# Reordering the recurrent block's second half in a one-core, two-block transformer kernel

## The reference, cut to what matters

```
u = x @ w_in
gate, rec = u[..., :D_RNN], u[..., D_RNN:]
rec = causal_depthwise_conv(rec, conv_w, conv_b)        # 4 taps
g = einsum('bsnd,nde->bsne', rec by 8 blocks of 128, w_gate) + b_gate
r = sigmoid(g[..., :128]);  i = sigmoid(g[..., 128:])
log_a = -8 * r * softplus(-lam);  a = exp(log_a)
b = sqrt(-expm1(2 * log_a)) * (i * rec)
h_t = a_t * h_(t-1) + b_t                               # scan over tokens
out = (gelu(gate) * h) @ w_out                          # then added to the residual
```

## Time and profile before

| | us |
|---|---|
| Median of three runs | 1183.83 |
| Profiled execution, its own time | 1185.08 |
| Span in the profile | 1183.3 |
| TensorE (PE) busy | 1170.0 (99%) |
| VectorE (DVE) busy | 819.0 (69%) |
| ScalarE (ACT) busy | 691.8 (58%) |
| GpSimd (POOL) busy | 89.3 (8%) |
| Mean granted TensorE clock | 0.999 |

### The profile page before, as it was taken

How to read it: one execution, slowest core, us unless ns; L and a number is a source line. 1 busy time by engine, 2 the same in 40 slices (tenths; PEclk the granted TensorE clock), 3 DMA queues, 4 the chain that set the end, 5 groups by cost and what they waited for, 6 DMA issues and landing times. The chain is left out here.

```text
span 1183.3 us, 25989 instructions
## 1 busy us (share of the span) xinstructions
PE 1170.0 (99%) x9738; PEld 1141.6 (96%) x9738; DVE 819.0 (69%) x1296; ACT 691.8 (58%) x1116; POOL 89.3 (8%) x97
## 2 busy tenths in 40 slices
PE   9999999999999999999999999999999999999998
PEld 8999999999998899999999999999999979999998
DVE  7767866666577877666668897665567677776543
ACT  6635765654455667665556986664447576666432
POOL 1000200000110020000120000000013222000000
PEclk9999999999999999999999999999999999999999
DMA  8532555556564336665664556666665424566663
GB/s 276 172 99 89 190 176 178 176 176 196 196 202 142 107 111 190 190 187 194 211 211 153 177 193 195 193 195 187 208 215 196 143 82 148 181 194 193 202 195 106
DMA packets 57577, 207.84 MB, mean 176 GB/s; under 512 B 6352, under 2 KB 7568, under 8 KB 57248
## 3 DMA queue, kind: packets, MB, share of 16 engines
q1 hardware_dynamic: 57136, 203.52, 54.3%
q0 software_dynamic: 288, 3.21, 0.7%
q10 hardware_dynamic: 80, 0.07, 0.0%
HBM read 205.66 MB, written 1.05 MB: 175 GB/s over the span
## 5 line engine op out<-in xcount | busy, mean ns | idle before, releaser
L1682 DVE TENSOR_TENSOR w_lo<-w_raw,w_hi 128x1024 fp32r<-128x1024 f32 x379 | 463.5, 1225 | 69.4 <-ACT w_hi L511 68.8
L511 ACT CAST w_hi<-w_raw 128x1024 fp32r<-128x1024 f32 x379 | 395.3, 1045 | 176.9 <-PE acc L1009 172.5
L1007 PE MATMUL acc<-x_hi,w_hi 128*128 128x256 f32 (+1 forms) x1688 | 479.2, 284 | 1.5 <-DVE w_lo L1682 1.1
L1008 PE MATMUL acc<-x_lo,w_hi 128*128 128x256 f32 (+1 forms) x1688 | 473.6, 281 | 0.0
L1009 PE MATMUL acc<-x_hi,w_lo 128*128 128x256 f32 (+1 forms) x1688 | 473.4, 280 | 0.0
L1007 PEld LDWEIGHTS acc<-x_hi,w_hi 128*128 128x128 f32 x1688 | 317.9, 188 | 5.4 <-DVE x_lo L1702 1.7
L1008 PEld LDWEIGHTS acc<-x_lo,w_hi 128*128 128x128 f32 x1688 | 317.8, 188 | 0.5
L1009 PEld LDWEIGHTS acc<-x_hi,w_lo 128*128 128x128 f32 x1688 | 317.8, 188 | 0.0
L1008 PE MATMUL acc<-m_lo,w_hi 128*128 128x256 f32 x512 | 141.3, 276 | 0.0
L1007 PE MATMUL acc<-m_hi,w_hi 128*128 128x256 f32 x512 | 141.3, 276 | 0.0
L1009 PE MATMUL acc<-m_hi,w_lo 128*128 128x256 f32 x512 | 141.3, 276 | 0.0
(11 more groups left out here) (370 smaller groups left out, 1671.2 us busy)
## 6 DMA issues: line engine op xcount, KB each, us to landing
w_raw<-weights SPq DMA_DIRECT2D x381, 512.0 KB, 4.2
bias<-bias_rows POOLq DMA_DIRECT2D x1, 2048.0 KB, 9.4
h<-hT SPq DMA_DIRECT2D x4, 272.0 KB, 4.5
bias<-bias_rows POOLq DMA_DIRECT2D x1, 1088.0 KB, 8.8
outT<-h SPq DMA_DIRECT2D x4, 256.0 KB, 4.6
con<-constants SPq DMA_DIRECT2D x1, 913.0 KB, 8.6
w_raw<-weights SPq DMA_DIRECT2D x2, 256.0 KB, 3.7
par<-cols SPq DMA_DIRECT2D x1, 84.0 KB, 2.0
```

The source lines that it names most:

```text
L511: nc.scalar.copy(w_hi[:, slot, :], w_raw[:, slot, :]).then_inc(hi_ready, 1)
L1007: nc.tensor.matmul(out, wh, xh[:, k, tok], start=first and n == 0, stop=False)
L1008: nc.tensor.matmul(out, wh, xl[:, k, tok], start=False, stop=False)
L1682: V.tensor_tensor(w_lo[:, slot, :], w_raw[:, slot, :], w_hi[:, slot, :].bitcast(F32), ALU.subtract)\
```

## The change

The orders of three pieces of program are changed; no operation is added, and of the gelu calls two (tiles 4 and 5, tiles 6 and 7) become one (tiles 4 to 7). The semaphore value that `gate_recurrence` waits for follows that.

- ScalarE: `tanh_root(1)` and the high part of unit 18 go ahead of `gelu(0, 4)` and the four `lead_out` behind it. The last gelu stands behind the high part of unit 21.
- VectorE: `drive(1)` and the eviction of y5 go ahead of the four `gate_recurrence`. The evictions of y6 and y7 stand between low parts `trail_out`. The low parts of units 20, 21 and 22 now stand one group of `source` and `recur` earlier in the order, and the gate products of tiles 4 and 5 stand ahead of the scans of tiles 6 and 7.

```diff
 ScalarE
             half_tanh(1)
+            tanh_root(1)
+            split_lru(18)
             gelu(0, 4)
             for n in range(4):
                 lead_out(n)
-            split_lru(18)
-            tanh_root(1)
             split_lru(19)
             decay(1)
             split_lru(20)
-            gelu(4, 6)
             split_lru(21)
-            gelu(6, 8)
-            lead_out(4)
-            lead_out(5)
+            gelu(4, 8)
             split_lru(22)
-            lead_out(6)
-            lead_out(7)
+            for n in range(4, 8):
+                lead_out(n)
             split_lru(23, 24, 25)
 VectorE
-                dve.wait_ge(s_("gelu_ready"), 1 if n < 4 else 2 if n < 6 else 3)
+                dve.wait_ge(s_("gelu_ready"), 1 if n < 4 else 2)
...
             normalise(4, 5, 6, 7)
+            drive(1)
+            evict("y5")
             for n in range(4):
                 gate_recurrence(n)
-            evict("y5")
             split_lru(18)
-            for n in range(4):
-                trail_out(n)
+            trail_out(0)
             evict("y6")
-            drive(1)
+            trail_out(1)
+            evict("y7")
             split_lru(19)
-            evict("y7")
+            trail_out(2)
+            trail_out(3)
+            split_lru(20)
             source(4)
             source(5)
             recur(4)
             recur(5)
-            split_lru(20)
+            split_lru(21)
             source(6)
             source(7)
+            gate_recurrence(4)
+            gate_recurrence(5)
             recur(6)
             recur(7)
-            gate_recurrence(4)
-            gate_recurrence(5)
-            split_lru(21)
+            split_lru(22)
+            trail_out(4)
+            trail_out(5)
             gate_recurrence(6)
             gate_recurrence(7)
-            trail_out(4)
-            trail_out(5)
-            split_lru(22)
             trail_out(6)
             trail_out(7)
             split_lru(23, 24, 25)
```

## The result

The changed kernel takes 1185.64 us in the median of 21 runs (1184.33 to 1187.76), the one before 1183.78 us in 21 runs beside them (1181.99 to 1186.45). The ratio is 1.0018, 95% interval 1.0012 to 1.0024: 2.1 us slower (1.4 to 2.8), where +2.4 was forecast. The profiled execution took 1186.75 us with a span of 1184.7.

What follows compares the result with a forecast made beforehand. TensorE, busy 1170.0 of 1183.3 us, was taken to bound the kernel, with VectorE feeding it here. VectorE's idle rising from 1.6 to 4.0 us gave +2.4 on the median 1183.83: 1186.2 us, range 1182 to 1189.5.

Steps and rivals of the forecast that it cites:

- What bounds: TensorE is nearly full and VectorE feeds it; removing a TensorE stall is worth nothing unless VectorE's stream also gets earlier.
- First half: Up to unit 18: VectorE waits 1.8 us for gelu, TensorE's two stalls become one of 3.8 us, net 0.1 us lost.
- Second half: Units 19 to 23: VectorE idles 1.1 us for w_hi 20 and 0.6 for w_hi 23; first adds to h at 698.86.
- The new stalls on TensorE: Waits of about 1.0 us ending at 693, 0.8 ahead of unit 23 and 0.8 at x tile 6.
- The forecast's last part: Expected profile; wrong if the add comes before 697, exp has no load, or no TensorE wait stands between 692 and 710.
- Rival C: TensorE's clock falls behind the 3.8 us wait; three slow stretches give +6.6 us, 1190.4 us; chance 0.03.
- Rival A: On ScalarE one table serves gelu and exp, so no load between; delay shrinks to +1.2, 1185.0 us; chance 0.12.
- B: The gain at unit 21 is kept, lr_lo 4 and w_lo 22 coming by 692.05; -0.4 us, 1183.4 us; chance 0.09.
- D: Late weights: landings of 5.8 us for units 26 and 27 add 1 to 2 us, 1187.7 us; chance 0.12.
- drain behind a table load: On ScalarE, about 1.38 us added to each table switch; the sum would be an estimated +3.8 us; not seen in the trace.
- the sum of 2.4: VectorE's idle in this stage goes from 1.6 to 4.0 us, and everything after is the same code: +2.4 us.

Runs made afterwards that it cites:

- e4: The kernel before with the evictions of y6 and y7 between its low parts and drive(1) behind them; ratio 1.0001 (0.9992 to 1.0010).
- e7: The same operations as the changed kernel in a new order on ScalarE and VectorE meant to leave VectorE no wait; 0.9992 against before (0.9983 to 1.0001).
- e1: The changed kernel with 14 products ones x ones in TensorE's wait for unit 18; ratio against before 1.0009 (1.0000 to 1.0018).
- e2: The kernel before with only the change's first half, up to the low part of lr 3; ratio 1.0016 (1.0007 to 1.0025).
- e6: e2 with 14 products ones x ones in TensorE's wait for unit 18; ratio against before 0.9998 (0.9989 to 1.0007).
- e3: The kernel before with only the change's second half: gelu(4, 8) in one call, low parts 20 to 22 earlier; ratio 1.0022 (1.0012 to 1.0031).
- e8: e7 with split_lru(28) moved behind the additions to h on both engines; ratio against before 0.9985 (0.9977 to 0.9994).

## Why the prediction was right

- **What bounds.** That a TensorE stall is worth nothing unless VectorE's stream gets earlier: shown by e4 (1.6 us of stall gone, no gain) and e7 (TensorE's wait grows from 1.8 to 2.4, the stretch is 1.1 us shorter).
- **First half.** gelu's end, the wait of 1.8 us (1.75), w_lo 18 (679.31 less the 0.3 us of the earlier start: 679.00) and unit 18's start (680.95 less 0.3, measured 680.65) were right to 0.1 us. The stall on y7 went.
- **Second half.** The wait for w_hi 20 was forecast as 1.1 (1.09), that for w_hi 23 as 0.6 (0.52). The first add to h came 26.46 us after y4's eviction, forecast 698.86 - 672.31 = 26.55. The low part of x tile 6: 36.96, forecast 34.72 + 2.4 = 37.1.
- **The new stalls on TensorE**, 1.0, 0.8 and 0.8 us, don't show in the changed kernel. The forecast's last part made that a sign of being wrong, and so this part of it failed: the time came out right, TensorE's path did not. With the clock held up (e1) the stalls are 0.99, 0.43 and 0.64. The second was over-sized, and by my own rows it should have read 0.9 (693.07 + 2.74 = 695.81 to 696.75): w_lo 23 began 0.1 us sooner than I chained it, unit 22 had itself lost about 0.2 us within, and a bracket counts from the last matmul's recorded end (0.28 us each), where I counted in steps of 0.114.
- **Rival C was the real miss in likelihood.** I gave the fall of the clock little weight because both waits of before had left it at 1.00. It fell, for 5.3 us and not 4, and cost TensorE 2.5 us, not 1.7. That such a fall would be covered by the waits behind it was right to 0.33 us, but with luck in the sizes: 2.5 us of low clock met 2.06 us of waits. In e2, with only 0.90 us of such waits behind it (0.63 and 0.27 in e6), the fall cost 0.9 us to the reciprocal (39.86 against 38.93 in e6). The kernel before's single execution was weak evidence: with the same 1.8 us wait the clock fell in e3 and e4.
- **Rival A** (no load between gelu and exp) is refuted by the row at 680.49, **B** by the wait of 0.99 us at unit 22 in e1. **D:** ScalarE waited 0.35 us for the load of w_hi 28 in the changed kernel, with no wait of VectorE behind it.
- The Trainium skill's drain behind a table load (ScalarE: Activation LUTs, "What ACT_TABLE_LOAD costs"), by which the sum would have been an estimated +3.8, is not in these traces: load 671.79, root 673.08, 1.29 us apart.
- **The span** of the profiled execution grew by 1.4 us only, for it was 0.3 us ahead at y4 and took 0.7 us less between 931 and 1010 us, where the code is the same; the sum of 2.4 stands against 2.1 timed.

## What to carry to other kernels

Where a feeding engine is nearly full, add up its idle time from a common start to the point where the fed engine needs it, and not the fed engine's stalls. Swapping two steps of one chain moves the wait to the other one unless the work between them covers both; in these runs the stretch got shorter only when VectorE's waits summed to less. Before reading a timed loss as that of one cause, compare executions with the same mean clock. Where TensorE must wait once for long, try idle products in the wait if nothing behind it covers a lower clock (e2 against e6).

## What the runs showed of the hardware

- The granted clock went to 0.50 (1.2 GHz) behind waits of 3.5 and 3.7 us (changed, e2), and of 1.8 us (e3, e4) and 2.4 us (e8) in their profiled executions; behind the same 1.8 us it stayed at 1.00 in the kernel before. It stayed low for 3 to 6 us of matmuls (3.0 in e3, 5.3 in the changed kernel, 5.9 in e2). Which waits bring it about isn't settled by these runs.
- In the executions of the changed kernel with mean clock 0.996 the span was 1184.1 us (7 of them), with 0.998 1182.6 (6), 1.5 us apart. The traces of this stage give the low clock 0.33 us (40.50 against 40.17). So they don't account for most of that difference; where it lies is open.
